# The first expert's gather on its own, and the gate tiles of the last two experts ahead of their down tiles

## The reference

```python
def _moe(h, w_router, b_router, w_gu, b_gu, w_dn, b_dn):
    logits = hf @ w_router + b_router               # 256 tokens, 32 experts
    top_val, top_idx = lax.top_k(logits, 4)
    gates = jax.nn.softmax(top_val, axis=-1)
    ...
    def run_block(args):                            # tokens toks of expert e
        xb = h_pad[toks]
        gu = xb @ w_gu[e] + b_gu[e]                 # 1024 -> 2048
        g, u = gu[:, :D_EXPERT], gu[:, D_EXPERT:]
        g = jnp.minimum(g, 7.0)
        u = jnp.clip(u, -7.0, 7.0)
        act = (u + 1.0) * (g * jax.nn.sigmoid(1.702 * g))
        return act @ w_dn[e] + b_dn[e]              # 1024 -> 1024
    ...                                             # times gate, summed per token
```

## Time and profile before

| | |
|---|---|
| median of 3 runs | 1605.26 us (1604.49 to 1605.91) |
| the profiled execution, its own time | 1601.7 us |
| its span, first to last instruction | 1599.9 us |
| PE busy | 1521.0 us (95%) |
| DVE, ACT busy | 453.6, 278.9 us |
| DMA queue of the weights (q1) | 511.29 MB, 78.9% of 16 engines' span |
| mean granted clock of TensorE | 0.998 |

### The profile page before, as it was taken

The page is one execution under the profiler, slowest core; times in us unless marked ns, Lnnn a source line. Parts: engine busy times, 40 slices in busy tenths (PEclk is TensorE's granted clock), DMA queues, the critical chain, the costliest instruction groups (busy, mean ns, idle before and its releaser), DMA issues.

```text
span 1599.9 us, 18309 instructions
## 1 busy us (share of the span) xinstructions
PE 1521.0 (95%) x7435; PEld 862.9 (54%) x7435; DVE 453.6 (28%) x967; ACT 278.9 (17%) x554; POOL 21.5 (1%) x43
## 2 busy tenths in 40 slices
PE   7999999999999999999999999999999999999997
PEld 6868787787887887733333333333333333233232
DVE  2444455523345651311121121112112111111111
ACT  1234114414232431210000000000000000000000
POOL 4000000000000000000000000000000000000000
PEclk9999999999999999999999999999999999999999
DMA  9833976445434443799999999999999999999996
GB/s 247 307 133 111 349 230 211 171 157 213 139 133 145 158 158 150 300 397 425 426 428 426 428 427 428 427 428 427 429 426 428 427 428 426 428 426 427 425 427 290
DMA packets 85272, 518.82 MB, mean 324 GB/s; under 512 B 5716, under 2 KB 9100, under 8 KB 60640
## 3 DMA queue, kind: packets, MB, share of 16 engines
q1 hardware_dynamic: 81744, 511.29, 78.9%
q0 software_dynamic: 2272, 3.04, 1.1%
q10 hardware_dynamic: 1200, 3.70, 0.7%
HBM read 516.39 MB, written 3.19 MB: 325 GB/s over the span
## 4 chain that ended last, share of the span: by engine, by line
PE 78%; DMA 14%; DVE 4%; issue 2%; ACT 1%; ACTq 0%; SPq 0%; DVEq 0%
PE psum L518 27%; PE psum L1169 20%; PE psum L1266 12%; DMA ring<-in_w_gu 9%; DMA w_down<-in_w_gu 5%; PE psum L1147 4%; PE psum L527 4%; PE psum L1156 2%; PE psum L1114 2%; PE psum L558 1%; PE psum L583 1%; PE psum L1254 1%; DVE hidden L2267 1%; DVE qk L1775 1%; PE psum L552 1%
## 5 line engine op out<-in xcount | busy, mean ns | idle before, releaser
L518 PE MATMUL psum<-spare,ring 128*128 128x256 f32 x1504 | 333.5, 382 | 3.2 <-ACT spare L1483 2.4
L518 PEld LDWEIGHTS psum<-spare,ring 128*128 128x128 f32 x1504 | 284.7, 191 | 48.7 <-issue 8.3
L1169 PE MATMUL psum<-ring,hg 128*64 128x512 f32 x1040 | 233.3, 596 | 6.4 <-DMA ring<-in_w_gu 6.4
L1169 PEld LDWEIGHTS psum<-ring,hg 128*64 128x64 f32 x1040 | 71.0, 137 | 155.2 <-issue 140.8
L1169 PE MATMUL psum<-w_down,hg 128*64 128x512 f32 x656 | 146.5, 596 | 5.9 <-DMA w_down<-in_w_gu 5.9
L2258 DVE TENSOR_SCALAR gu<-psum 128x512 f32<-128x512 f32 x32 | 22.1, 692 | 326.7 <-PE psum L1169 326.7
L2270 DVE TENSOR_TENSOR o_slot<-psum,gain_rows 128x512 f32<-128x512 f32 x32 | 22.1, 691 | 319.0 <-PE psum L1266 319.0
L1169 PEld LDWEIGHTS psum<-w_down,hg 128*64 128x64 f32 x656 | 44.7, 137 | 99.3 <-issue 88.1
L1266 PE MATMUL psum<-w_down,hiddenT 128*64 128x512 f32 x352 | 78.0, 595 | 9.4 <-ACT hiddenT L1738 7.2
L1266 PE MATMUL psum<-ring,hiddenT 128*64 128x512 f32 x352 | 78.0, 595 | 8.3 <-issue 8.3
L1732 ACT ACTIVATE putT<-psum 128x256 f32<-128x256 f32 x32 | 12.3, 383 | 380.4 <-PE psum L1176 380.4
(11 more groups left out here) (416 smaller groups left out, 1422.5 us busy)
## 6 DMA issues: line engine op xcount, KB each, us to landing
ring<-in_w_gu SPq DMA_DIRECT2D x65, 2048.0 KB, 28.2
w_down<-in_w_gu SPq DMA_DIRECT2D x41, 2048.0 KB, 28.3
ring<-in_w_in SPq DMA_DIRECT2D x24, 2048.0 KB, 9.1
w_down<-in_w_dn SPq DMA_DIRECT2D x22, 2048.0 KB, 28.8
ring<-in_w_dn SPq DMA_DIRECT2D x22, 2048.0 KB, 31.7
ring<-in_w_ada SPq DMA_DIRECT2D x12, 2048.0 KB, 8.1
spare<-in_w_gu SPq DMA_DIRECT2D x11, 2048.0 KB, 28.3
nine<-in_w_gu SPq DMA_DIRECT2D x11, 2048.0 KB, 29.8
```

The source lines that it names most:

```text
L518: mm = pe.matmul(bank[0:m, c * T:(c + 1) * T], w[:, k, c0 + c * P:c0 + c * P + m], src[:, k, :], start=(i == 0), stop=(i == k_n - 1))
L1169: mm = pe.matmul(psum[half * CAP:(half + 1) * CAP, loop_bank(4 + part), :], hg[:, k, side, :], w[:, c0:c0 + 512], start=False, stop=(k == ...
```

## The change

There are two parts. At the head, `gather` takes a slice of sides. Side 0 of the first pair is gathered ahead of expert 0's gate tiles, side 1 between its gate tiles 0 and 1. DVE signals `picked` after each side, and ACT copies each side into `hg` for itself; so `picked` counts one more and `hg` two more from there on. At the tail, the tiles of the last two experts are loaded and used in another order: eight gate tiles, then the down tiles of expert 30, then those of expert 31. PE, ACT and DVE are written out for this pair in that order; SP's last 36 loads are written out instead of looped.

```diff
+    LAST_M = NE - 2 - 6 * (SIXES - 1)
+    LAST_TILES = [(0, 0), (0, 1), (0, 2), (0, 3), (1, 0), (1, 1), (1, 2), (1, 3), (0, 4), (0, 5), (1, 4), (1, 5)]
...
         t = 6 * m + j
+        if last_pair(i, m):
+            t = 6 * LAST_M + LAST_TILES.index((m - LAST_M, j))
         return t % SLOTS, 4 * i + t // SLOTS
...
-        def gather(width, first_bank=4):
+        def gather(sides, first_bank=4):
+            width = sides.stop - sides.start
...
-                                       pick[:, b, 0:width, :], start=(b == 0), stop=(b == NB - 1))
+                                       pick[:, b, sides, :], start=(b == 0), stop=(b == NB - 1))
...
             if j == 1:
                 pe.wait_ge(ev("passes"), 1)
+                pe.wait_ge(ev("hg"), 4)
...
-                if first and j != 1:
-                    pe.wait_ge(ev("hg"), 1 if j == 0 else 2)
+                if first and j == 0:
+                    pe.wait_ge(ev("hg"), 1)
...
+                if j == 0 and first:
+                    pe.wait_ge(ev("picked"), 2)
+                    pe.wait_ge(ev("hg"), 2)
+                    gather(slice(1, 2), 6)
...
         pe.wait_ge(ev("picked"), 1)
-        gather(2, 6)
+        gather(slice(0, 1), 6)
...
+        pe.wait_ge(ev("hg"), 6 * i + 10)
+        gates_up(NE - 2, 0, i, LAST_M)
+        add_up(1)
+        turn_hidden(NE - 2)
+        gates_up(NE - 1, 1, i, LAST_M + 1, put_here=False)
+        down(NE - 2, i, LAST_M)
+        turn_hidden(NE - 1)
+        pe.wait_ge(ev("o_slot"), NE - 1)
+        put(1)
+        add_up(0)
+        down(NE - 1, i, LAST_M + 1)
         pe.wait_ge(ev("o_slot"), NE)
         add_up(1, last=True)
...
+            if last_pair(i, m):
+                dm, j = LAST_TILES[6 * (m - LAST_M) + j]
+                m, n = LAST_M + dm, NE - 2 + dm
             load(i, m, n, j)
...
-        gathered(1, first_bank=6)
+        gathered(1, slice(0, 1), first_bank=6)
+        gathered(3, slice(1, 2), first_bank=6)
...
-        expert(NE - 2, 0)
-        expert(NE - 1, 1)
+        put_copy(NE - 2, 0)
+        gate_sigmoid(NE - 2)
+        turn_copy(NE - 2)
+        gate_sigmoid(NE - 1)
+        turn_copy(NE - 1)
+        put_copy(NE - 1, 1)
...
                 ins = pick_only(side, b, side)
-        ins.then_inc(ev("picked"), 1)
+            ins.then_inc(ev("picked"), 1)
...
-        pair(NE - 2, last=True)
+        hidden_of(NE - 2)
+        dve.wait_ge(ev("hidden_turned"), NE - 1)
+        hidden_of(NE - 1)
+        slot_out(NE - 2)
+        dve.wait_ge(ev("added"), NE - 1)
+        slot_out(NE - 1)
```

More of the change, by code:

```diff
@@ L399, in weight_slot, with last_pair @@
         return tile, ev(f"tile_full{s}"), 0
+    LAST_M = NE - 2 - 6 * (SIXES - 1)
+    LAST_TILES = [(0, 0), (0, 1), (0, 2), (0, 3), (1, 0), (1, 1), (1, 2), (1, 3), (0, 4), (0, 5), (1, 4), (1, 5)]
+    def last_pair(i, m):
+        return isinstance(i, int) and i == SIXES - 1 and m is not None and m >= LAST_M
     def expert_slot_of(i, m, j):
@@ L1209, in down_bias, with gates_up @@
                               start=False, stop=False, skip_group_check=True)
-        def expert(n, side, i, m, before, first=False, gather_after=None):
+        def gates_up(n, side, i, m, first=False, put_here=True):
             if not first:
@@ L1231, in expert @@
                         mm.then_inc(ev("gu_done"), 1)
-                if j == 0 and not first:
+                if j == 0 and first:
+                    pe.wait_ge(ev("picked"), 2)
+                    pe.wait_ge(ev("hg"), 2)
+                    gather(slice(1, 2), 6)
+                if j == 0 and put_here and not first:
                     pe.wait_ge(ev("o_slot"), n)
@@ L1242, in expert, with turn_hidden @@
                 down_bias()
[L1243 to L1248, removed]
+        def turn_hidden(n):
             pe.wait_ge(ev("hidden"), n + 1)
-            if first:
-                pe.wait_ge(ev("todo"), 1)
             for c in range(4):
@@ L1255, in expert, with down @@
             mm.then_inc(ev("hidden_turned"), 1)
+        def down(n, i, m):
             pe.wait_ge(ev("putT"), n + 1)
@@ L1268, in expert @@
                 mm.then_inc(ev(f"down_done{j}"), 1)
+        def expert(n, side, i, m, before, first=False, gather_after=None):
+            gates_up(n, side, i, m, first)
+            if before is not None:
+                add_up(before)
+            if gather_after is not None:
+                pe.wait_ge(ev("picked"), gather_after)
+                pe.wait_ge(ev("u_in"), n + 1)
+                gather(slice(0, 2))
+            if first:
+                pe.wait_ge(ev("todo"), 1)
+            turn_hidden(n)
+            down(n, i, m)
         for k in (6, 7):
@@ L1275, in _ @@
         pe.wait_ge(ev("picked"), 1)
-        gather(2, 6)
+        gather(slice(0, 1), 6)
         expert(0, 0, 0, 0, None, first=True)
-        expert(1, 1, 0, 1, 0, gather_after=2)
+        expert(1, 1, 0, 1, 0, gather_after=3)
         with nc.Fori(0, SIXES - 1, engines=[mybir.EngineType.PE], hint_back_edge=True) as i:
             for q in range(3):
-                pe.wait_ge(ev("hg"), 6 * i + 2 * q + 4)
+                pe.wait_ge(ev("hg"), 6 * i + 2 * q + 6)
                 expert(6 * i + 2 * q + 2, 0, i, 2 * q + 2, 1)
[L1284 to L1287, removed]
+                expert(6 * i + 2 * q + 3, 1, i, 2 * q + 3, 0, gather_after=3 * i + q + 4)
+        i = SIXES - 1
+        for q in range(2):
+            pe.wait_ge(ev("hg"), 6 * i + 2 * q + 6)
             expert(6 * i + 2 * q + 2, 0, i, 2 * q + 2, 1)
-            expert(6 * i + 2 * q + 3, 1, i, 2 * q + 3, 0, gather_after=3 * i + q + 3 if q < 2 else None)
+            expert(6 * i + 2 * q + 3, 1, i, 2 * q + 3, 0, gather_after=3 * i + q + 4)
+        pe.wait_ge(ev("hg"), 6 * i + 10)
[9 more added lines that the diff above has]
+        down(NE - 1, i, LAST_M + 1)
         pe.wait_ge(ev("o_slot"), NE)
@@ L1295, in _ @@
                 with pe.Fori(first, first + TOGETHER) as i:
-                    pe.wait_ge(ev("picked"), i + PAIRS + 1)
-                    gather(1)
-                    pe.wait_ge(ev("hg"), 2 * i + 2 * PAIRS + 2)
+                    pe.wait_ge(ev("picked"), i + PAIRS + 2)
+                    gather(slice(0, 1))
+                    pe.wait_ge(ev("hg"), 2 * i + 2 * PAIRS + 4)
                     expert(i + NE, 0, i, None, None)
@@ L1369, in _ @@
             load_after(0, 1, 1, j)
-        with sp.Fori(0, SIXES) as i:
+        with sp.Fori(0, SIXES - 1) as i:
             for m in range(2, 8):
@@ L1373, in _ @@
                     load_after(i, m, 6 * i + m, j)
+        for m in range(2, 8):
+            for j in range(6):
+                load_after(SIXES - 1, m, 6 * (SIXES - 1) + m, j)
         sp.wait_ge(ev("todo"), 1)
@@ L1720, in _, with gathered @@
         ins.then_inc(ev("gate_exp"), 1)
-        def gathered(n, width=2, first_bank=4):
+        def gathered(n, sides=slice(0, 2), first_bank=4):
             for part in range(2):
@@ L1726, in gathered, with put_copy, gate_sigmoid, turn_copy @@
                 bank = psum[:, loop_bank(first_bank + part), :].rearrange("p (k e s) -> p k e s", k=4, e=2)
-                act.activation(hg[:, 4 * part:4 * part + 4, 0:width, :], bank[:, :, 0:width, :], ACT.Copy)\
+                act.activation(hg[:, 4 * part:4 * part + 4, sides, :], bank[:, :, 0:sides.stop - sides.start, :], ACT.Copy)\
                     .then_inc(ev("hg"), 1)
-        def expert(n, side, gather_after=None):
+        def put_copy(n, side):
             act.wait_ge(ev("turned"), n + 1)
             act.activation(putT[:, side, :], psum[:, loop_bank(7), 0:T], ACT.Copy).then_inc(ev("putT"), 1)
+        def gate_sigmoid(n):
             act.wait_ge(ev("g_in"), n + 1)
             act.activation(hidden[:, 0, :], gu[:, 0, :], ACT.Sigmoid, scale=1.702).then_inc(ev("g_sig"), 1)
-            if gather_after is not None:
-                gathered(gather_after)
+        def turn_copy(n):
             act.wait_ge(ev("hidden_turned"), n + 1)
@@ L1739, in expert @@
                 .then_inc(ev("hiddenT"), 1)
-        gathered(1, first_bank=6)
+        def expert(n, side, gather_after=None):
+            put_copy(n, side)
+            gate_sigmoid(n)
+            if gather_after is not None:
+                gathered(gather_after)
+            turn_copy(n)
+        gathered(1, slice(0, 1), first_bank=6)
+        gathered(3, slice(1, 2), first_bank=6)
         act.wait_ge(ev("turned"), 1)
@@ L1746, in _ @@
         expert(0, 0)
-        expert(1, 1, gather_after=3)
+        expert(1, 1, gather_after=5)
         with act.Fori(1, PAIRS - 1) as i:
             expert(2 * i, 0)
-            expert(2 * i + 1, 1, gather_after=2 * i + 3)
-        expert(NE - 2, 0)
-        expert(NE - 1, 1)
+            expert(2 * i + 1, 1, gather_after=2 * i + 5)
+        put_copy(NE - 2, 0)
[4 more added lines that the diff above has]
+        put_copy(NE - 1, 1)
         act.wait_ge(ev("todo"), 1)
@@ L2253, in _, with hidden_of @@
```

(11 more changed lines are left out.)

2 lines of the change are left out of this document (1 added, 1 removed).

## The result

The changed kernel takes 1614.75 us (median of 5 runs, 1612.72 to 1618.98), the kernel before 1605.26 us: 9.5 us more by the medians. I had forecast 1607.7 us and a range up to 1609.6. So it is slower, by at least four times my sum of 2.4 us. The mean granted clock was 0.992 or 0.993 in all five runs; in the profiled execution of the kernel before it was 0.998.

What follows compares the result with a forecast made beforehand. The prediction took the saturated DMA queue as the bound, fed late by PE's head: +3.3 us there, -0.9 us at the tail, +2.4 us on 1605.26 gives 1607.7 us, range 1604.6 to 1609.6.

Steps and rivals of the forecast that it cites:

- my sum of 2.4 us: Whole kernel: head's delay of 3.3 us less the tail's gain of 0.9 us.
- The bound and where time can be lost: Expert loop: DMA queue is always full, so only empty-queue time at the head and PE's work after the last landings count.
- E: SP's load issue after the first half of expert 0's down product, at 703.98; claimed just in time, without slack.
- The gather's price at full clock: Head: 32 records of 64 columns cost 0.110 us each, 3.5 us for one gather, bounds 3.4 and 3.7.
- The first gather: Side 0, ahead of tile 0: 0.2 us saved on 4.38 us, with the clock back at full from about 677.7.
- The clock rival: Head: narrow gather makes TensorE's clock fall again, PE loses 1.7 us ahead of E, +4.1 us in total; chance 0.16.
- The tail: Last two experts: reordered tiles start the last down product 6.7 instead of 7.64 us after the tenth tile, gain 0.9 us.
- SP's and PE's code: SP's last six experts written out: issues run some 35 us ahead of landing, covering any code fetch, so no cost.
- A: SP's load issue at 684.31, the first of the head's slot releases; forecast 0.2 us earlier, at 684.1.

Runs made afterwards that it cites:

- experiment 7: Tail's change, first gather old, all 15 gathers in the loop split into two of 64 columns: 1637.08 us, ratio 1.0204 to the kernel before.
- experiment 10: Whole change plus three filling matrix products in PE's waits at the router and in expert 0: 1606.29 us against 1604.66 for the kernel before.
- experiment 9: Kernel before with the tail's change, old gather and three filling products (router's wait, two in expert 0): 1600.85 us against 1604.66, ratio 0.998.
- experiment 1: Head's change alone, with the old tail and SP's loop: 1613.29 us against 1604.03 for the kernel before, ratio 1.0071.
- experiment 3: Head's change with the first gather at 128 columns again, the second still at 64: 1609.36 us, ratio 1.0035 to the kernel before.
- experiment 6: Head's change, old tail, plus one 512-column filling product in the router's wait: 1609.1 us, ratio 1.0026 to the kernel before.
- experiment 5: Tail's change, old gather, plus one 512-column filling product in PE's wait for the router: 1603.83 us, ratio 0.9992 to the kernel before.
- experiment 8: Kernel before with only the 512-column filling product in the router's wait added: 1603.23 us, ratio 0.9996.
- experiment 2: Tail's change alone, with the old 128-column gather: 1603.21 us against 1604.03 for the kernel before, ratio 0.9998.
- experiment 11: Tail's change with three filling products, plus four 64-column products in each of four late experts: 1603.15 us, ratio 0.9992 to the kernel before.

## Why the prediction was wrong

**The bound and where time can be lost: right.** The head's delay reached the end unchanged. E is 11.2 us later in the profile and the tenth tile of the last pair 11.1. The rule that a slower PE doesn't move the end in the middle of the loop holds only within PE's margin of some 2.7 us in a pair: 3.5 more in each pair cost 33 us (experiment 7).

**The gather's price at full clock: right within 0.2 us.** I took 3.5, it is 3.71 (0.116 us a record, my upper bound), and 3.84 with the joints around it (experiment 10 against 9). That half the columns cost as much was the step that I had put most care into, and it held.

**The first gather: the step that failed.** "Of the 32 records some 6 run at half clock and 26 at full" took the return of the clock at 677.7 from the trace of before, as if it were an event of its own. It depended on the work that the change replaces. With 64 columns all 32 records ran at half clock (6.85 us instead of my 4.2) and most of tile 0 too (5.96 instead of 3.58): 5.05 us above my sum. Experiments 1 and 3 differ in the columns alone and show it.

**The clock rival: right in the suspect, wrong in the mechanism and the size.** I had it at 0.16 and +1.7 us, as a new fall out of a full clock. But a full clock survives narrow gathers (experiments 6 and 7), and what they do is keep it low once it is low. My argument against, that at 699 PE was busy 0.41 of a microsecond and the clock stayed, was weak as well: at the same place the clock did fall in the changed kernel and in experiments 5, 6 and 8 (1.4 to 1.6 us each), so that its standing in one trace was partly luck.

The Trainium skill ("TensorE: Matmul & The Clock Gate", section "Part 1: The HAM clock gate (the "warmup" mystery)") says that sustained matmul activity releases the throttle and that instructions aren't counted. In this case that wasn't enough, and the measurement decides: PE is listed busy 1.00 of each microsecond in windows from 676 on, and the clock stays at 0.50 to 688.9. I had read the page as leaving this open, and should have given it more than 0.16.

**The tail: right.** 0.9 predicted, 0.84 in experiment 2 (7.64 to 6.80).

**SP's and PE's code: a term put at nothing that may not be.** I asked only whether SP's longer code would delay its loads, and gave PE's no price. With more PE instructions SP's last wait was 3.9 instead of 2.1 us (experiment 11), and in the changed kernel 4.2; that the code is the cause, and what it costs in time, stays open. SP's written-out loads alone show nothing (2.1 us in experiment 2).

**The sum as it should have been**, from the gather's start on: 4.85 to A, 3.71 for the second gather and 0.2 around it, 1.42 for the second fall, -0.8 for the tail, +2.1 in SP's last wait: 11.5 in the profiled execution. The ratio gives 11.4, the medians 9.5. Part of this gap is the trace that it is set against: its old head took 27.74 us, that of experiments 2 and 7 some 28.5. My step from the profiled execution to the median was off too: I added the 3.6 us by which the kernel before's median lies above it; for the changed kernel that difference is 0.2.

## What to carry to other kernels

Ahead of a stage that is bound by a saturated DMA queue, the few microseconds of TensorE work between the first tile and the release that finds the queue empty count in full, while work in the middle counts only beyond TensorE's margin over the DMA: look for the window with 0 GB/s and for the issue that ends it. When a matmul with a 128x128 weight load is split by columns, count both parts at the full price. Whenever a change makes such records narrower, look at the granted clock where they stand: right behind a fall they can hold TensorE at 1.2 GHz, and a product of 512 columns in the wait ahead of it is cheap, but here it was only of use with the next thin place filled too.

## What was unexpected in the hardware

- Records of 64 columns behind 128x128 weight loads kept the clock at half for 10.2 us (experiment 1) and 13.6 us (the changed kernel), with PE listed as busy throughout; the same number of records with 128 columns let it rise after 3.4 us (experiment 3, and the old head in its traces). Under a full clock 7.3 us of them, 15 times, did nothing to it.
- A fall of the clock that is prevented at one place came at the next thin one: 25 us later, about 3.4 us long as the first, at 1.4 to 1.6 us. With both filled, there was none. The kernel before has single runs too with a mean clock of 0.994 to 0.996 and up to 1612 us; where their clock was lost isn't known.
- With 16 small products more in PE's code, placed where PE waits anyway, SP's last wait for the output was 3.9 us instead of 2.1 in the trace. A gain or loss in time can't be told from the runs.
